# Scan step of a two-block layer: the state tile written in two quarters instead of whole through a mask

## Chip, cores and metric

The kernel runs on one core of a Trainium2 chip. The metric is the device time of one execution in microseconds; the kernel before has a median of 3163.56 us over three runs (3161.9 to 3165.33). One further execution was profiled; every row below is from it. Engine names are those of the profile: PE multiplies matrices (PEld is its weight load), DVE, ACT and POOL work elementwise, SP issues transfers.

## The reference, cut to what matters

The whole computation is two blocks of a network (feed-forward layers, convolutions, gating, retention). The change lies in one layer of the second block, the RWKV scan of 12 heads of width 64 over 768 tokens, in two directions:

```
def rwkv7_scan(r, w, k, v, kk, bb, s0, reverse):
    def step(s, inp):
        r_t, w_t, k_t, v_t, kk_t, b_t = inp
        sa = jnp.einsum('bhij,bhj->bhi', s, kk_t)
        s = s * w_t[:, :, None, :] - sa[..., None] * b_t[:, :, None, :] + v_t[..., None] * k_t[:, :, None, :]
        return s, jnp.einsum('bhij,bhj->bhi', s, r_t)
    ...
    s, ys = lax.scan(step, s0, xs, reverse=reverse)
```

Each head carries a 64 x 64 state `s` from token to token.

## The kernel before

`even_scan_phase` does the scan by chunks of 128 tokens (`CH`). Two heads share the 128 partitions: one head on partitions 0 to 63, the other on 64 to 127 (`SIDES`). There are six such pairs (`b` = 0 to 5, `RB` = 6), each with six chunks (`k` = 0 to 5, `NCH` = 6) and two directions (`d` = 0 and 1), so 36 steps of `step(b, k, between)` with both directions in each. The order of work is written out by hand: every engine has its own `step`, with the parts of direction 0 and 1 one after the other, and between them slots (`between(0)` to `between(5)`) into which the preparation of later pairs is put.

The state of a pair and direction is `V.sc` ("gathered" in the trace, 128 x 64: both heads stacked) and, for the products, `V.s` (a "state" tile in SBUF, 128 x 128): the two 64 x 64 blocks stand on its diagonal and the two other quarters are zero. On PE, `right` (L2900) and `read` (L2927) of the next step multiply with `V.s`. In the trace "state" is also the name of the PSUM tile `V.low`.

On DVE a step ends in this order: `join` for both directions (L3315, writes `V.x`), slot 3, `add` of direction 0 (L3325 on), `turn` of direction 0 and of direction 1 (L3321, a copy from PSUM to the half `early` of `V.t`: partitions 0 to 63 in direction 0, 64 to 127 in direction 1), `add` of direction 1, slots 4 and 5. `add` has three operations: the new `V.sc` (L3332, or a copy in L3334 at `k` = 0), the sum of the outputs (L3337), and after a wait for both the spread into `V.s` (L3339). PE's `close` (L2886) needs both `turn` copies of DVE and ACT's copy `y` (L3108); ACT's `close` (L3114) follows it, and PE's `take` of the next step (L2829) waits for that. PE's `tokens`, three copies on ACT (L3097 to L3100), and then `take` on DVE (L3296, "br") come next.

POOL works beside this for the next pairs: `prepare` with products of 128 x 768 (L2721), and `invert`, a chain of small products on 96 partitions (L2709, L2712), each waiting for the one before. It works for pairs 1 to 5, so it is nearly idle in the last pair.

Of the kernel before, what the change touches and what calls it, by code (L numbers as in the profile page):

```python
# [9 lines left out]
ALU = mybir.AluOpType  # L10
# [54 lines left out]
def at(i, n):  # L65

    return bass.ds(i, n)
# [2376 lines left out]
def even_scan_phase(K):  # L2444
# [7 lines left out]
    SIDES = (slice(0, 64), slice(64, 128))  # L2452
# [9 lines left out]
    with phase(K, "tables", "cleared", "late_ready", "late_out", *(f"gate_in{i}" for i in range(4)), "gate_hi", "gate_lo", "gate_lo_dve", "gate_done", "pp", "pa", "pd", "pq", "omk", "lw", "low_ps", "low_copied", "low_out0",  # L2462
# [23 lines left out]
        U = []  # L2486
# [23 lines left out]
        def heads(ap):  # L2510
            return ap.rearrange("p (a c) -> p a c", a=1).broadcast_to([P, 2, ap.shape[1]])

        def cols(d, k):
            return slice(ORDER[d][k] * CH, (ORDER[d][k] + 1) * CH)

        def total(b, k, signals, extra=0):

            return b * (NCH * signals) + (k * signals + extra)
# [53 lines left out]
        with nc.Block() as block:  # L2572
# [648 lines left out]
            def _(dve):  # L3221
# [103 lines left out]
                def add(b, k, d):  # L3325
                    O, V, way = B[b % 3], U[d], cols(d, k)
                    ch = ORDER[d][k]
                    dve.wait_ge(V.ps, total(b, k, PS, 4))
                    fresh = V.low[:, 3 * P:3 * P + 64]
                    if k:  # L3330
                        was = ORDER[d][k - 1]
                        new = dve.scalar_tensor_tensor(V.sc[:], V.sc[:], O.wlast[:, d, was:was + 1], fresh, ALU.mult, ALU.add)  # L3332
                    else:
                        new = dve.tensor_copy(V.sc[:], fresh)  # L3334
                    new.then_inc(V.ds, 1)
                    oc = u[:, at(b, 1), way].rearrange("p a t -> p (a t)")
                    dve.tensor_tensor(oc, oc, V.low[:, 2 * P:3 * P], ALU.add).then_inc(V.ds, 1)  # L3337
                    dve.wait_ge(V.ds, total(b, k, DS, 2))
                    dve.scalar_tensor_tensor(V.s.rearrange("p (h c) -> p h c", h=2), heads(V.sc), O.wlast[:, d, ch:ch + 1],  # L3339
                                             K.bd64.rearrange("p (h c) -> p h c", h=2), ALU.mult,  # L3340
                                             ALU.mult).then_inc(V.ds, 1)

                def begin():
                    dve.wait_ge(S.gate_done, GATES_DONE)
# [7 lines left out]
                def step(b, k, between):  # L3352
                    nxt = following(b, k)
                    take, keys, cross, join, turn = chunk_parts(nxt) if nxt else (lambda d: None,) * 5
                    if k == 0:
                        if b:
                            for d in range(2):
                                dve.wait_ge(U[d].ds, total(b, 0, DS))
                        dve.wait_ge(S.pd, prep("dve", b, "bonus"))
                    take(0)  # L3360
                    take(1)
                    between(0)
                    keys(0)
                    keys(1)
                    between(1)
                    cross(0)
                    cross(1)
                    between(2)
                    join(0)
                    join(1)  # L3370
                    between(3)
                    add(b, k, 0)
                    turn(0)
                    turn(1)
                    add(b, k, 1)
                    between(4)
                    between(5)
# [1341 lines left out]
```

## Time and profile before

| | |
|---|---|
| median of the runs | 3163.56 us |
| the profiled execution | 3161.93 us, of it span 3160.1 us |
| PE busy | 2982.9 us (94%), 22801 instructions |
| DVE busy | 2205.5 us (70%), 3864 instructions |
| ACT, POOL busy | 1387.2 us (44%), 1590.3 us (50%) |
| scan steps | 433 us, from 2241 to 2674 us of the span |
| L3339, the operation replaced | 72 times, 35.0 us |

The busy share of PE is high over the whole span, but many of its instructions in the scan are small products whose modelled lengths overlap. Which engine sets the pace of the scan is read from the waits and the order of time, not from the shares.

### The profile page before, as it was taken

The page shows a single profiled execution, that of the slowest core. Times are in us where ns is not written, and L with a number is a line of the kernel's source. Part 1 is how long each engine was busy: PE and PEld are TensorE (multiplying, and loading weights), DVE is VectorE, ACT ScalarE, POOL GpSimd, SP SyncE. Part 2 cuts the span into 40 slices and gives each one's busy share as a digit, 9 for nine tenths or more (in the row PEclk, how much of TensorE's full clock was granted, in tenths as well). Part 3 has the DMA queues.
Part 4 walks back from the last instruction along what each step waited for, and adds up shares of the span by engine and source line. Part 5 has one row for each costly group of instructions (what it writes and reads, how often), then busy time and mean ns, then how long its engine had stood idle before and what let it go on. Part 6 is the DMA issues. An engine that isn't in the chain of part 4 may idle for free. (4 is left out here: it accounts for less than half of the span.)

```text
span 3160.1 us, 57423 instructions
## 1 busy us (share of the span) xinstructions
PE 2982.9 (94%) x22801; PEld 2548.7 (81%) x22801; DVE 2205.5 (70%) x3864; ACT 1387.2 (44%) x2651; POOL 1590.3 (50%) x1197
## 2 busy tenths in 40 slices
PE   5999999899999999999999999999888899989998
PEld 4999876689987999877799888887666676778887
DVE  6998488799956999642799866447677764774443
ACT  4555235455524545234454524236444433444333
POOL 3776442367644775343477533224776660243333
PEclk8999999999999999999999999999899999999999
DMA  6565532246553564432345444214222243222222
GB/s 206 174 211 165 158 85 66 60 142 213 179 159 109 178 204 141 151 86 66 92 134 154 137 144 141 60 57 115 60 57 53 55 117 98 66 75 71 80 67 60
DMA packets 641459, 367.05 MB, mean 116 GB/s; under 512 B 107903, under 2 KB 634133, under 8 KB 640689
## 3 DMA queue, kind: packets, MB, share of 16 engines
q1 hardware_dynamic: 633216, 351.57, 38.0%
q10 hardware_dynamic: 6640, 10.49, 1.1%
q8 instruction: 176, 2.88, 0.4%
q0 software_dynamic: 1344, 1.44, 0.2%
q14 instruction: 83, 0.67, 0.1%
HBM read 334.27 MB, written 24.97 MB: 114 GB/s over the span
## 5 line engine op out<-in xcount | busy, mean ns | idle before, releaser
L270 POOL TENSOR_TENSOR w_lo<-w_raw,w_hi 128x1024 fp32r<-128x1024 f32 (+1 forms) x181 | 433.6, 2397 | 822.8 <-ACT w_hi L262 758.3
L262 ACT ACTIVATE w_hi<-w_raw 128x1024 fp32r<-128x1024 f32 (+1 forms) x172 | 175.1, 1018 | 364.1 <-PE acc L335 263.7
L1288 PE MATMUL scaled<-h_terms,h 128*128 128x256 f32 x1856 | 260.5, 283 | 0.0
L1288 PEld LDWEIGHTS scaled<-h_terms,h 128*128 128x128 f32 x1856 | 239.4, 192 | 0.0
L335 PE MATMUL acc<-h_terms,w_hi 128*128 128x512 f32 x584 | 220.0, 395 | 4.7 <-POOL w_lo L270 3.9
L978 DVE SCALAR_TENSOR_TENSOR ada_part<-ada_raw,c_act,ada_part 128x256 f32<-128x256 f32 x432 | 210.7, 488 | 16.1
L335 PE MATMUL acc<-hid,w_hi 128*128 128x512 f32 x528 | 206.1, 390 | 0.0
L335 PE MATMUL lat<-h,w_slots 128*128 128x512 f32 x672 | 199.5, 396 | 4.6 <-ACT plain L3967 4.0
L335 PE MATMUL acc<-h_terms,w_lo 128*128 128x512 f32 x520 | 203.3, 391 | 0.0
L668 DVE TENSOR_TENSOR scaled<-z,x 128x512 f32<-128x512 f32 x36 | 41.9, 1165 | 184.9 <-ACT z L609 184.9
L1135 POOL TENSOR_TENSOR h<-z,h 128x512 fp32r<-128x512 f32 x80 | 108.3, 1354 | 105.0 <-ACT h L1167 105.0
L335 PEld LDWEIGHTS lat<-h,w_slots 128*128 128x128 f32 x672 | 125.1, 188 | 33.1 <-ACT plain L3967 5.8
L1290 PE MATMUL scaled<-h_terms,h 128*128 128x256 f32 x928 | 149.2, 283 | 0.0
L270 POOL TENSOR_TENSOR w_slots<-w_raw,w_slots 128x1024 fp32r<-128x1024 f32 x28 | 68.9, 2459 | 159.5 <-ACT w_slots L262 153.1
L1135 POOL TENSOR_TENSOR w_lo<-w_sums,w_hi 128x512 fp32r<-128x512 f32 x72 | 93.7, 1301 | 103.4 <-ACT w_hi L1167 103.4
L1167 ACT ACTIVATE h<-w_raw 128x512 fp32r<-128x512 f32 x156 | 96.9, 624 | 103.5 <-PE scaled L1290 93.5
L335 PE MATMUL acc<-h,w_hi 128*128 128x512 f32 x408 | 134.9, 398 | 0.0
L335 PEld LDWEIGHTS acc<-h_terms,w_hi 128*128 128x128 f32 x584 | 110.1, 189 | 28.7 <-POOL w_lo L270 4.2
L1290 PEld LDWEIGHTS scaled<-h_terms,h 128*128 128x128 f32 x928 | 128.1, 192 | 0.0
L335 PEld LDWEIGHTS acc<-hid,w_hi 128*128 128x128 f32 x528 | 99.6, 189 | 19.4
L335 PEld LDWEIGHTS acc<-h_terms,w_lo 128*128 128x128 f32 x520 | 97.9, 188 | 20.9
L744 DVE SCALAR_TENSOR_TENSOR ada_part<-ada_raw,c_act,ada_part 128x256 f32<-128x256 f32 x240 | 109.8, 488 | 5.7
(789 smaller groups left out, 8826.4 us busy)
## 6 DMA issues: line engine op xcount, KB each, us to landing
w_raw<-in_ffn_w SPq DMA_DIRECT2D x240, 512.0 KB, 4.5
ada_raw<-in_ada_w SPq DMA_DIRECT2D x88, 1024.0 KB, 5.6
w_raw<-in_od_w_in SPq DMA_DIRECT2D x32, 512.0 KB, 4.1
w_raw<-in_ffn_w SPq DMA_DIRECT2D x32, 384.0 KB, 3.5
w_raw<-in_ev_w_in SPq DMA_DIRECT2D x22, 512.0 KB, 3.9
image<-inverse_wait SPq DMA_DIRECT2D x144, 64.0 KB, 2.1
first_ada<-in_ada_w SPq DMA_DIRECT2D x8, 1024.0 KB, 12.5
w_raw<-in_ab_w_in SPq DMA_DIRECT2D x16, 512.0 KB, 4.0
```

The source lines that it names most:

```text
L262: act.activation(K.w_hi[:, first % SPLIT, 0:tiles, :], K.raw[:, first % RAW, 0:tiles, :], ACT.Copy).then_inc(K.hi_ready, 1)
L270: pool.tensor_tensor(K.w_lo[:, first % SPLIT, 0:tiles, :], K.raw[:, first % RAW, 0:tiles, :], K.w_hi[:, first % SPLIT, 0:tiles, :].bitcast ...
L335: mm = pe.matmul(out, w[:, slot, k, :], moving(ap, k, tokens), start=first and k == 0 and p == 0, stop=last and k == tiles - 1 and p == le ...
L668: dve.tensor_tensor(S.tp[b % 2][:], K.z[:, b, :], K.x[:, b, :], ALU.mult).then_inc(S.crossed, 1)
L744: ins = dve.scalar_tensor_tensor(out, raw[:, k, :], col, part[:, v, :], ALU.mult, ALU.add)
L978: ins = dve.scalar_tensor_tensor(out, K.ada_raw[:, q % ADA, k, :], col, S.ada_part[:, v, :], ALU.mult, ALU.add)
L1135: pool.tensor_tensor(lo_of(t, p), full_of(t, p), hi_of(t, p).bitcast(F32), ALU.subtract).then_inc(S.lo, 1)
L1167: act.activation(hi_of(t, p), full_of(t, p), ACT.Copy).then_inc(S.hi, 1)
L1288: pe.matmul(out_of[p], hi_of(t, p)[:, k, :], moving[p][:, part, k, :], start=k == 0 and part == HI, stop=False)
L1290: mm = pe.matmul(out_of[p], lo_of(t, p)[:, k, :], moving[p][:, HI, k, :], start=False, stop=k == KH - 1)
```

## The change

The one masked operation L3339 on 128 x 128 elements (gathered state, taken twice, times decay, times the mask of ones and zeros `K.bd64`) becomes two operations on 64 x 64 elements, one for each head, each with its own decay and without a mask. In the first step of the scan each direction's `V.s` is set to zero once, and the first spread waits for that.

```diff
                     new.then_inc(V.ds, 1)
+                    if not b and not k:
+                        dve.memset(V.s[:], 0.0).then_inc(S.cleared, 1)
                     oc = u[:, at(b, 1), way].rearrange("p a t -> p (a t)")
                     dve.tensor_tensor(oc, oc, V.low[:, 2 * P:3 * P], ALU.add).then_inc(V.ds, 1)
                     dve.wait_ge(V.ds, total(b, k, DS, 2))
-                    dve.scalar_tensor_tensor(V.s.rearrange("p (h c) -> p h c", h=2), heads(V.sc), O.wlast[:, d, ch:ch + 1],
-                                             K.bd64.rearrange("p (h c) -> p h c", h=2), ALU.mult,
-                                             ALU.mult).then_inc(V.ds, 1)
+                    if not b and not k:
+                        dve.wait_ge(S.cleared, len(U) + d + 1)
+                    for a in SIDES:
+                        spread = dve.tensor_scalar(V.s[a, a], V.sc[a, :], O.wlast[a, d, ch:ch + 1], None, ALU.mult)
+                    spread.then_inc(V.ds, 1)
```

DVE around an `add` of both directions, before (pair 0, `k` = 4; `local40` and `local41` are `V.ds` of the two directions, `local30` and `local31` are `V.pa`, on which PE signals):

```order
L3337 TENSOR_TENSOR u<-u,state_561 128x128
L3339 SCALAR_TENSOR_TENSOR state<-gathered,w_last,const 128x128 [waits local40]
L3321 COPY t<-chunk_560 64x2x64 [waits local30]
L3321 COPY t<-chunk_571 64x2x64 [waits local31]
L3332 SCALAR_TENSOR_TENSOR gathered<-gathered,w_last,state_572 128x64 [waits local37]
L3337 TENSOR_TENSOR u<-u,state_572 128x128
L3339 SCALAR_TENSOR_TENSOR state<-gathered,w_last,const 128x128 [waits local41]
L3280 SCALAR_TENSOR_TENSOR x_context<-x_context,params,u 128x768 [waits local15]
L3296 TENSOR_TENSOR br<-chunk_560,masks 128x256 [waits local32]
```

The same place now:

```order
L3339 TENSOR_TENSOR u<-u,state_561 128x128
L3344 TENSOR_SCALAR state<-gathered,w_last 64x64 [waits local40]
L3344 TENSOR_SCALAR state<-gathered,w_last 64x64
L3321 COPY t<-chunk_560 64x2x64 [waits local30]
L3321 COPY t<-chunk_571 64x2x64 [waits local31]
L3332 SCALAR_TENSOR_TENSOR gathered<-gathered,w_last,state_572 128x64 [waits local37]
L3339 TENSOR_TENSOR u<-u,state_572 128x128
L3344 TENSOR_SCALAR state<-gathered,w_last 64x64 [waits local41]
L3344 TENSOR_SCALAR state<-gathered,w_last 64x64
L3280 SCALAR_TENSOR_TENSOR x_context<-x_context,params,u 128x768 [waits local15]
L3296 TENSOR_TENSOR br<-chunk_560,masks 128x256 [waits local32]
```

Nothing has moved; one operation has become two in each direction, and the second of them waits for nothing. Two `turn` copies stand behind the first pair of operations, and L3280 and `br` behind the second. Elsewhere the order is the same on every engine, but for the two clearing operations in the first step.

## Rows read from the trace of the kernel before

**Rows 1.** Busy time of each engine in the stretch of the scan steps

```profile
core 0: us, PE busy (x) PEld busy (x) DVE busy (x) ACT busy (x) POOL busy (x), PEclk, DMA share, GB/s
...
2241.00:2674.00 433.00, 378.61 (x6507) 284.87 (x6501) 288.42 (x682) 199.44 (x656) 257.65 (x353) 0.97 0.28 65
```

**Rows 2.** Waits in 2241 to 2673: waiter, releaser, total us, times, longest us

```profile
DVE br L3296 <- ACT tok L3100: 57.5, 54, 2.9
...
PE chunk L2886 <- DVE t L3321: 18.0, 31, 1.5
...
PEld state L2900 <- issue: 5.4, 29, 0.3
```

**Rows 3.** L3339 over the run: ns min/median/max; then busy us, mean ns

```profile
L3339 DVE SCALAR_TENSOR_TENSOR state<-gathered,w_last,const x72: 351/353/1678, 2241.5 to 2673.4; 128x128 f32<-128x128 f32 x72
...
L3339 DVE SCALAR_TENSOR_TENSOR state<-gathered,w_last,const 128x128 f32<-128x128 f32 x72 | 35.0, 486 | 2.6
```

**Rows 4.** Timeline (start us, us) of a step without POOL: DVE, then PE

```profile
2617.81 0.35 DVE L3339 SCALAR_TENSOR_TENSOR state<-gathered,w_last,const 128x128 f32<-128x128 f32 x1
2618.08 0.60 DVE L3321 COPY t<-chunk 64x128 f32<-64x128 f32 x2
...
2618.50 0.74 PE L2886 MATMUL chunk<-t,y 64*64 64x64 f32 x8 [0.21 <-DVE t L3321]
```

**Rows 5.** Pairs of DVE operations, timeline; and their mean ns by shape

```profile
2331.13 0.52 DVE L3315 TENSOR_TENSOR x<-image,chunk 128x128 f32<-128x128 f32 x2 [1.55 <-PE chunk L2864]
...
L3321 DVE COPY t<-chunk 64x128 f32<-64x128 f32 x72 | 20.5, 285 | 1.6 <-PE chunk L2877 0.4
...
L3315 DVE TENSOR_TENSOR x<-image,chunk 128x128 f32<-128x128 f32 x72 | 18.7, 287 | 35.7 <-PE chunk L2864 35.4
```

**Rows 6.** Single-input multiplications by a column elsewhere: busy us, mean ns

```profile
L3742 DVE TENSOR_SCALAR own_weights<-select,fac 128x32 f32<-128x32 f32 x2 | 0.4, 238 | 0.0
...
L3758 DVE TENSOR_SCALAR dft_lat<-sq,fac 128x256 f32<-128x256 f32 x1 | 0.3, 348 | 0.0
```

**Rows 7.** Timeline, a step with POOL's small products: DVE, POOL, PE

```profile
2254.10 0.61 DVE L3339 SCALAR_TENSOR_TENSOR state<-gathered,w_last,const 128x128 f32<-128x128 f32 x1
2254.63 0.60 DVE L3321 COPY t<-chunk 64x128 f32<-64x128 f32 x2
...
2253.96 0.60 POOL L2712 TENSOR_TENSOR w_raw<-w_raw,x 96x210 f32<-96x210 f32 x1
2254.64 0.59 POOL L2709 TENSOR_TENSOR x<-w_raw 96x220 f32<-96x220 f32 x1
...
2255.05 0.74 PE L2886 MATMUL chunk<-t,y 64*64 64x64 f32 x8 [0.97 <-DVE t L3321]
```

**Rows 8.** Timeline, a step with POOL's large products: DVE, then POOL

```profile
2292.35 1.56 DVE L3339 SCALAR_TENSOR_TENSOR state<-gathered,w_last,const 128x128 f32<-128x128 f32 x1
...
2295.64 2.57 DVE L3280 SCALAR_TENSOR_TENSOR x_context<-x_context,params,u 128x768 f32<-128x768 f32 x1
2298.13 0.74 DVE L3296 TENSOR_TENSOR br<-chunk,masks 128x256 f32<-128x256 f32 x2
...
2291.94 1.82 POOL L2721 TENSOR_TENSOR q_r_rate<-q_r_rate,x 128x768 f32<-128x768 f32 x1
2293.72 3.68 POOL L2721 TENSOR_TENSOR q_r_rate<-q_r_rate,u 128x768 f32<-128x768 f32 x2
```

**Rows 9.** Timeline of small operations outside the scan: DVE, then POOL

```profile
303.47 1.78 DVE L648 TENSOR_SCALAR fac<-mods 128x8 f32<-128x8 f32 x1
305.36 2.24 DVE L651 TENSOR_TENSOR fac<-fac,params 128x8 f32<-128x8 f32 x1
...
299.21 6.02 POOL L270 TENSOR_TENSOR w_lo<-w_raw,w_hi 128x768 fp32r<-128x768 f32 x1 [7.64 <-ACT w_hi L262]
...
305.19 2.38 POOL L270 TENSOR_TENSOR w_lo<-w_raw,w_hi 128x1024 fp32r<-128x1024 f32 x1
```

**Rows 10.** DVE's timeline behind the second direction's L3339 at k = 1

```profile
2335.32 1.76 DVE L3261 RECIPROCAL x_context<-x_context 128x128 f32<-128x128 f32 x2
2336.99 1.43 DVE L3243 TENSOR_TENSOR_SCAN q_r_rate<-dft_feat,q_r_rate 128x256 f32<-128x256 f32 x2
2338.34 0.90 DVE L3296 TENSOR_TENSOR br<-chunk,masks 128x256 f32<-128x256 f32 x2
```

## The prediction, made before the changed kernel was timed

> **What bounds the kernel now.** I read the busy time by stage first. The change touches only the scan steps: 433 us, in which DVE is busy 288 us [rows 1]. It is neither full nor idle, so the waits decide. In them PE's closing product L2886 waits in 31 of 35 steps for DVE's `turn` copy L3321, 18.0 us in all, while PE's first product with the spread state (L2900) never waits for DVE, only for 0.3 us at most of its own issue [rows 2]. So the spread state is always ready in time; what its making costs is that it stands in DVE's queue ahead of the `turn` copies. In a step without POOL the operation L3339 takes 0.35 us, the copies start 0.27 us after it began, and L2886 starts 0.42 us after them [rows 4]. With POOL at work L3339 takes 0.61 us, the copies start at 0.53 and L2886 at 0.95, again 0.42 after the copies [rows 7]. PE, then ACT, then PE's `take` and ACT's copies follow, and DVE itself waits 54 times for those copies before `br` [rows 2]. Time that direction 0's `add` gains or loses on DVE therefore goes into the step nearly whole. Direction 1's comes behind the copies and counts only where DVE has no rest before `br`.
>
> **What one operation costs now.** Alone 0.351 us; over 72 of them 35.0 us, so 35.0 - 72 x 0.351 = 9.7 us are waiting inside the operation [rows 3]. Of this 6.9 us fall to direction 0 (18 operations above 0.4 us, six of these above 0.7) and 2.75 us to direction 1. The cause is seen in the timelines: POOL's product ends at 2254.56, L3339 at 2254.71 [rows 7]; POOL's ends at 2293.76, L3339 at 2293.91 [rows 8]. Each time DVE's operation ends 0.15 us after POOL's: it has to wait until POOL is done, then streams its 128 columns. POOL starts its next product 0.08 us after the end of a small one [rows 7], and 0.04 us before the end of a large one [rows 8].
>
> **What two operations cost, alone.** The nearest rows for a single-input multiplication by a column are 0.238 us for 32 columns and 0.348 us for 256 [rows 6], half a ns a column; for 64 columns that is 0.25 us. (Bounds: 0.238 and 0.285, the latter a copy out of PSUM [rows 5].) Can the second start before the first has ended? Two `join` products of 0.287 us, both on all partitions, take 0.52 us together, so the second starts 0.05 us before the first ends; two `turn` copies of 0.285 us, the first written to the upper, the second to the lower 64 partitions, take 0.60 us, so there it starts 0.03 us after [rows 5 and 4]. The new pair changes halves as the `turn` copies do, and the first `turn` copy behind it changes back. I take the second case for both borders: 0.25 + 0.03 + 0.25 + 0.03 = 0.56 us from the start of the pair to the next operation, against 0.27 now: **+0.29 us** each time. By the first case it would be about 0.40, so +0.13.
>
> The Trainium skill, "VectorE: DVE Perf Modes", section "Two Vector instructions with no wait between them", states this as a rule: an instruction whose start quadrant (group of 32 partitions) differs from that of the last input or output in the same memory starts only when every earlier one has finished. The two pairs of rows agree, and by it both borders are held, as taken above; without it the sum below would be some 6 us less.
>
> **What two operations cost beside POOL.** The new ones read one tensor, L3339 read two. Do they still wait for POOL? Outside the scan a single-input multiplication of only 8 columns, L648, started at 303.47 and took 1.78 us; POOL's product ended at 305.23, L648 at 305.25. Behind it, after a wait for it, stands L651, again 8 columns: POOL had started its next product at 305.19, and L651 took 2.24 us, until 307.60, POOL's ending at 307.57 [rows 9]. So a small single-input operation is held up as well, and of two in a row **each is held up by a product of its own**: POOL takes its turn in between. In the new pair this does the following. The first ends 0.05 us after POOL's product (32 half-rate columns in place of 0.15 us); the second starts 0.03 later, when POOL has started its next one, and waits for its end, P later. Beside small products the next operation starts at end + 0.08 + P + 0.05 + 0.03, against end + 0.07 now: +0.09 + P. I put the pair in the place of each of the 72 operations in the timeline, with POOL's products as they lie there:
> - direction 0, 18 steps with POOL quiet or its product just over: 18 x 0.29 = 5.2 us;
> - direction 0, 14 steps with small products behind, P from 0.28 to 0.65 us (0.59 in [rows 7]), mean 0.53: 14 x 0.62 = 8.7 us;
> - direction 0, 4 steps with 1.82 us products behind [rows 8]: 4 x 1.81 = 7.3 us;
> - direction 1, only in the steps of pairs 0 to 3 where DVE has no rest before the next thing that is waited for: at `k` = 1, where reciprocals, scans and `br` follow without a gap [rows 10], 4 x 0.61 = 2.4; at `k` = 4, where `br` follows L3280 without one [rows 8], 4 x 1.91 = 7.7; at `k` = 5 4 x 0.29 = 1.2. Together 11.3 us. In the other 24 steps DVE waits for ACT before `br`, and that wait hides it; were the cover gone, at 0.29 each it would be 7 us more.
> - clearing: two writes of 128 columns, each under the 0.35 us of an operation that reads as many [rows 3], once: 0.3 us. The extra wait is on DVE's own clearing, with an operation in between.
>
> Sum: 5.2 + 8.7 + 7.3 + 11.3 + 0.3 = 32.8 us. Not all of it reaches the end: in some steps ACT is late by itself, and POOL's preparation does not move along, so a later step finds fewer products in its way. No row has this share; I take eight tenths, 26 us, with six tenths and the full sum (20 and 33) as ends. Against the profiled execution that is 3161.93 + 26 = 3188; that execution lies 1.6 us under the median of the runs, so I forecast **3190 us**.
>
> **The rivals.**
> *Held up once.* DVE's second operation might take its turn before POOL's next product: POOL's start and the second operation's fall together, at end + 0.08. Then every pair costs 0.29: 48 x 0.29 = 13.9, by the same share some 11 us: 3175. Against it stands L651 [rows 9], though POOL had there a start of 0.17 us.
> *Not held up at all.* The two lose the second tensor, and if that is what POOL collides with, the waiting of 9.7 us goes. Direction 0: 36 x 0.29 - 6.9 = 3.5; direction 1 in the 12 steps: 3.5 - 2.65 = 0.9; clearing 0.3: +4.7 us, 3168, not to be told from no change. L648 speaks against it [rows 9].
> The Trainium skill, "SBUF — State Buffer", section "Who interferes with whom", says that a DVE instruction with at most one SBUF input does not contend with GpSimd outside the two-port modes, and that single-input multiplications can enter such a mode and then take the shared pair for the whole instruction. The 0.5 ns a column of rows 6 (two elements in a cycle of the page's 0.96 GHz) speaks for that mode here.
> *Faster.* Not held up and not held at the change of halves either: about 0.20 us a pair decides it, since 48 pairs then give back 9.6 us in all. At two starts 0.17 us apart (0.34 in all, +0.07): 48 x 0.07 - 6.9 - 2.65 = -6 us, 3157. Both the copies of rows 5 and L648 would have to mislead.
>
> **How the numbers follow.** A measurement of this kernel tells about 0.2%, 6.3 us, from no change. Held up twice 0.66 (3180 to 3203), held up once 0.13 (3172 to 3180), not held up 0.13 (3164 to 3172), faster 0.05, and more than the full sum 0.03. The third case is within 0.2% but for 0.01 below it. Slower 0.82, same 0.12, faster 0.06. The range from 3167 to 3203 leaves out the faster case, the lower end of the case not held up and the tail above.
>
> **What would show it.** In the profile after, L3344 has 144 operations; alone 0.25 us; beside POOL some of up to 1.9 us, and their sum well over 35 us (near 36 + 30). In a quiet step `turn` starts 0.56 us after the pair. L2886 waits for L3321 for some 35 us in place of 18.0. The scan's stretch grows from 433 to about 459 us, and nothing outside it changes. Wrong it would be if no operation of L3344 is over 0.3 us (not held up), if only every first is (held up once), or if the longer pair stands while the stretch does not grow: then the wait for L3321 was not the one that counts.

## The result and the profile after

The changed kernel takes 3183.96 us (median of four runs, 3183.31 to 3186.17) against 3164.18 us before (four runs, 3161.9 to 3165.33): ratio 1.0066, 95% interval 1.0054 to 1.0079, so 19.8 us slower. The profiled execution took 3183.31 us, span 3181.5 us.

The replaced operation in the profile after, first by its summary over the run (ns min/median/max), then by busy us and mean ns, answering [rows 3]:

```profile
L3344 DVE TENSOR_SCALAR state<-gathered,w_last x144: 246/254/1764, 2244.8 to 2696.6; 64x64 f32<-64x64 f32 x144
```
```profile
L3344 DVE TENSOR_SCALAR state<-gathered,w_last 64x64 f32<-64x64 f32 x144 | 62.5, 434 | 3.6
```

Alone an operation takes 0.25 us, as forecast from [rows 6]. All 144 take 62.5 us in place of 35.0; 62.5 - 144 x 0.25 = 26.5 us of it are waiting, against 9.7 before.

A quiet step after, DVE and then PE (start us, us), answering [rows 4]:

```profile
2638.70 0.52 DVE L3344 TENSOR_SCALAR state<-gathered,w_last 64x64 f32<-64x64 f32 x2
2639.25 0.61 DVE L3321 COPY t<-chunk 64x128 f32<-64x128 f32 x2
```
```profile
2639.68 0.74 PE L2886 MATMUL chunk<-t,y 64*64 64x64 f32 x8 [0.49 <-DVE t L3321]
```

The copies start 0.55 us after the pair (0.27 before), PE's closing product 0.43 us after them, having waited 0.49 (0.21 before).

A step with POOL's large products after: DVE's two operations one by one, then POOL, answering [rows 8]:

```profile
2299.06 1.64 DVE L3344 TENSOR_SCALAR state<-gathered,w_last 64x64 f32<-64x64 f32 x1
```
```profile
2300.72 1.75 DVE L3344 TENSOR_SCALAR state<-gathered,w_last 64x64 f32<-64x64 f32 x1
```
```profile
2298.86 1.80 POOL L2721 TENSOR_TENSOR q_r_rate<-q_r_rate,x 128x768 f32<-128x768 f32 x1
2300.62 3.56 POOL L2721 TENSOR_TENSOR q_r_rate<-q_r_rate,u 128x768 f32<-128x768 f32 x2
```

POOL's product ends at 2300.66, the first operation at 2300.70. The second starts at 2300.72, when POOL has begun its next at 2300.62. The last row is two POOL products; by half of its 3.56 us the first of them ends at some 2302.4, and the second operation ends at 2302.47. So each operation was held up by a product of its own.

Waits in 2241 to 2700 after (total us, times, longest), answering [rows 2]:

```profile
PE chunk L2886 <- DVE t L3321: 36.4, 31, 3.4
...
POOL x L2721 <- DVE x_context L3261: 16.5, 4, 10.0
...
PEld state L2900 <- issue: 6.4, 29, 0.3
```

PE's closing product waits 36.4 us for the copies in place of 18.0; the product with the state tile still waits for nothing but its own issue. POOL now waits 16.5 us for DVE's reciprocals; before it was 1.9.

Where the 21.4 us between the spans lie: from the first to the last `add` of direction 0 the scan takes 450.5 us in place of 431.1, +19.4. It starts 3.2 us later (2244.27, before 2241.05), ahead of any changed operation, and what follows is 1.2 us shorter. In the twelve kernels below the same place lies between 2240.97 and 2249.46, so that start is not an effect of the change. Outside the scan the executions of these kernels take from 2729.0 us (before: span 3160.1 less the 431.1 in the table) to 2735.6 (psum) and 2739.8 (the pair in the other order), so a few us between two totals can lie there; the table shows the scan alone. The table sums the steps of pairs 0 to 3 by `k`, then pairs 4 and 5, each from one `add` of direction 0 to the next in the profiled executions (us); the kernels of the last five columns are described below.

| steps | before | changed | pair_d0 | pair_d1 | psum | late_after | on_act |
|---|---|---|---|---|---|---|---|
| k = 0 | 50.1 | 51.7 | 51.9 | 50.6 | 51.4 | 50.0 | 50.3 |
| k = 1 | 54.9 | 62.3 | 63.7 | 58.8 | 57.3 | 65.0 | 53.8 |
| k = 2 | 53.2 | 54.2 | 54.5 | 52.6 | 52.5 | 52.7 | 60.3 |
| k = 3 | 46.7 | 43.1 | 43.6 | 42.5 | 46.7 | 39.5 | 42.4 |
| k = 4 | 57.7 | 67.1 | 66.4 | 66.2 | 49.9 | 76.1 | 47.8 |
| k = 5 | 59.4 | 61.0 | 57.6 | 56.2 | 59.0 | 59.2 | 52.2 |
| pair 4 | 63.9 | 64.3 | 65.7 | 63.6 | 63.6 | 61.5 | 63.3 |
| pair 5 | 45.3 | 46.8 | 46.8 | 45.4 | 47.2 | 44.9 | 48.2 |
| sum | 431.1 | 450.5 | 450.1 | 435.7 | 427.6 | 448.9 | 418.2 |

### The profile page after: what moved, and what is told of

Read it like the earlier page. It is cut to its first block and busy times, and to the rows that moved or that the text cites. A ratio compares the mean times of both kernels' runs of the same rounds, so it can differ in the third digit from the quotient of the medians.

```text
span 3181.5 us, 57499 instructions
## 1 busy us (share of the span) xinstructions
PE 2992.3 (94%) x22801; PEld 2556.1 (80%) x22801; DVE 2235.8 (70%) x3938; ACT 1388.4 (44%) x2651; POOL 1587.4 (50%) x1197
## 3 DMA queue, kind: packets, MB, share of 16 engines
q0 software_dynamic: 1344, 1.44, 0.2%
## 5 line engine op out<-in xcount | busy, mean ns | idle before, releaser
L335 PEld LDWEIGHTS acc<-hid,w_hi 128*128 128x128 f32 x528 | 99.7, 189 | 19.4
```

The costliest lines, as they stand in the source:

```text
L335: mm = pe.matmul(out, w[:, slot, k, :], moving(ap, k, tokens), start=first and k == 0 and p == 0, stop=last and k == tiles - 1 and p == le ...
```

## The experiments

My theory: each of the two operations is held up by a product of POOL, and these hold-ups and 0.28 us of issue lengthen the step through the copies behind them. The rivals: that two operations cost by their issue alone; that the place in the queue is what counts; that TensorE's clock is part of it. Ratios are to the kernel before, run beside each.

**Away from POOL: the operand from PSUM.**

```diff
-                        spread = dve.tensor_scalar(V.s[a, a], V.sc[a, :], O.wlast[a, d, ch:ch + 1], None, ALU.mult)
+                        spread = dve.tensor_scalar(V.s[a, a], fresh[a, :], O.wlast[a, d, ch:ch + 1], None, ALU.mult)
```

> Both operations of the pair kept, but they read the chunk's new part from PSUM in place of the gathered state in SBUF (the state carried over from earlier chunks is left out of the spread tile). Theory that the pair is held up because it reads SBUF through what it shares with POOL: no operation is over 0.33 us, pair to copy 0.62 us everywhere, against 0.55 quiet and up to 3.4 beside POOL in the changed kernel. Sum against the kernel before: 36 x 0.35 - 6.9 + 12 x 0.35 - 2.65 = +7 us, 3171 (3166 to 3175). Rival, that two operations one behind the other are what costs by their issue and the waits behind: 3184 as the changed kernel, or above.

3164.77 us, ratio 1.0008 (0.9999 to 1.0017). The 144 operations over the run:

```profile
L3344 DVE TENSOR_SCALAR state<-state,w_last x144: 275/284/293, 2246.6 to 2675.6; 64x64 f32<-64x64 f32 x144
```

Each takes 0.03 us more than in the changed kernel and none is over 0.293 us, beside the same POOL work. Two operations, one behind the other, and almost nothing is lost: without hold-ups by POOL the loss is gone. What two cost alone is still there (pair 5, with POOL quiet, takes 47.2 us in place of 45.3), and it is given back at k = 4, where the four steps shrink to 49.9 us, below the 57.7 before. The hold-ups of the old masked operation are gone there too; by my sum that would be some 2.4 us, and L3280 takes 1.75 to 1.94 us there in place of 2.57. The time lies 6 us under what I expected, most of it at k = 4; why L3280 comes out shorter I did not test. The Trainium skill, "VectorE: DVE Perf Modes", section "Why PSUM operands drop a tier", says that the mode that reads through both SBUF ports is impossible with a PSUM operand; the trace agrees with that, with 293 ns at most against 1764, but does not show the mode itself.

**One operation in place of two.**

```diff
-                    for a in SIDES:
-                        spread = dve.tensor_scalar(V.s[a, a], V.sc[a, :], O.wlast[a, d, ch:ch + 1], None, ALU.mult)
+                    spread = dve.tensor_scalar(V.s[:, 0:64], V.sc[:], O.wlast[:, d, ch:ch + 1], None, ALU.mult)
```

> One single-input multiplication of all 128 partitions by 64 columns in the place of the pair; it writes only the left half of the state tile, so the right head's block is left out of the computation. Held-up-once-for-each-operation theory: it takes 0.25 us alone and can be held up by one product of POOL only; it ends 0.1 us earlier than the masked operation both alone and beside POOL, and the copies behind it start 0.17 us after it when POOL is quiet. Time 3160 (3157 to 3164). Rival, that the single-input mode beside POOL is what costs, however many operations there are: some operations over 1 us remain in the steps with small products, time 3172 or more.

3160.43 us, ratio 0.9994 (0.9985 to 1.0003).

```profile
L3343 DVE TENSOR_SCALAR state<-gathered,w_last 128x64 f32<-128x64 f32 x72 | 28.7, 399 | 2.6
```

Waiting: 28.7 - 72 x 0.25 = 10.7 us, as the masked operation's 9.7 and far from 26.5. One operation is held up as one was before; a quiet step takes 9.86 us in place of 9.96. The number of operations makes the loss, not their kind.

**A third operation.**

```diff
-                    for a in SIDES:
-                        spread = dve.tensor_scalar(V.s[a, a], V.sc[a, :], O.wlast[a, d, ch:ch + 1], None, ALU.mult)
+                    for a, c in zip((*SIDES, SIDES[0]), (*SIDES, SIDES[1])):
+                        spread = dve.tensor_scalar(V.s[a, c], V.sc[a, :], O.wlast[a, d, ch:ch + 1], None, ALU.mult)
```

> A third operation of the same kind behind each pair; it writes a quarter of the state tile that has to stay zero, so the result of the scan is another. Theory that each operation of its own is held up by one product of POOL: a quiet pair grows from 0.52 to 0.79 us, beside POOL the third ends one product later (1.1 to 1.7 us, 3.4 to 5.2), the operation's waiting over all is 1.5 to 1.7 times that of the changed kernel (26.5 us), and the time grows by about as much again as the second did: 3200 (3195 to 3208). Rival, that POOL is held up no more than twice since it has then caught up: only 72 x 0.27 us of issue, by the share of 0.6: 3192 or less.

3202.51 us, ratio 1.0123 (1.0108 to 1.0138): 39.6 us over the kernel before, twice the 19.8 of the pair.

```profile
L3344 DVE TENSOR_SCALAR state<-gathered,w_last 64x64 f32<-64x64 f32 x216 | 97.1, 449 | 4.7
```
```profile
2298.66 3.78 DVE L3344 TENSOR_SCALAR state<-gathered,w_last 64x64 f32<-64x64 f32 x3
```

Waiting: 97.1 - 216 x 0.25 = 43.1 us, 1.6 times that of the pair. At k = 4 direction 0's three take 5.3 to 5.4 us in pairs 1 to 3, one product more than two. In pair 0 (the row of 3.78 us) the first was held up by none (0.26 us) and the other two by one product each (1.75 and 1.74); in direction 1 of pairs 0 to 3 one of the three went free each time. In a quiet step the three take 0.78 us. So "one product each" is what most of these rows show, with exceptions.

**One direction at a time.** The pair in direction 0 or 1, the masked operation in the other:

```diff
+                    if d == 0:
                         for a in SIDES:
                             spread = dve.tensor_scalar(V.s[a, a], V.sc[a, :], O.wlast[a, d, ch:ch + 1], None, ALU.mult)
+                    else:
+                        spread = dve.scalar_tensor_tensor(...)
```

> The pair of operations in direction 0 alone, the masked operation kept in direction 1. The prediction's sum gives direction 0 21.3 of 32.8 us; the changed kernel's +19.8 us is 0.6 of the sum, so by the same share 13 us here: 3176. Rival, that direction 1 costs nothing because DVE waits before br anyway: the whole +20, 3183.

> The pair in direction 1 alone. By the sum 11.3 of 32.8 us, with the same share +7 us: 3170. Rival, direction 1 hidden: 3163. What is left over or missing when both halves are added is what the two directions hide or cause in one another.

Direction 0 alone: 3184.55 us, ratio 1.0068 (1.0053 to 1.0082), +21.7 us, all of the loss. Direction 1 alone: 3168.59 us, ratio 1.0018 (1.0009 to 1.0027), +5.7 us. Both rivals have half the truth: direction 1's pair is not hidden by itself, yet it adds nothing to direction 0's. At k = 4 either one lengthens the four steps from 57.7 to some 66 us, and both together to 67.1. The traces show why. With direction 1's pair alone, in 2241 to 2700:

```profile
PE prep L2772 <- DVE x_context L3280: 6.5, 4, 1.9
```

L2772 is PE's product for the next pair. At k = 4 it stands in PE's queue ahead of the `take` (L2829) that goes on with the scan, and it needs what L3280 writes. That `take` follows it without a gap in all four steps of the kernel before, the changed one and these two, and `br` had ended at least 0.9 us earlier: `br` is not what the step waits for there. Direction 1's pair makes L3280 late; direction 0's makes PE itself late, since the closing product waits for the copies. L2772 starts when the later of the two is done. With direction 0's pair alone it never waits for L3280 at k = 4, with both it waits 2.2 us in three steps. So the two delays cover each other.

**The pair in other orders.** First the lower half before the upper one (`for a in SIDES[::-1]`), then both on the upper half:

```diff
                     for a in SIDES:
-                        spread = dve.tensor_scalar(V.s[a, a], V.sc[a, :], O.wlast[a, d, ch:ch + 1], None, ALU.mult)
+                        spread = dve.tensor_scalar(V.s[SIDES[0], a], V.sc[SIDES[0], :], O.wlast[SIDES[0], d, ch:ch + 1], None, ALU.mult)
```

> The pair in the other order: the lower 64 partitions first, the upper ones last, so that direction 0's turn copy, which writes the upper ones, changes no half. Theory that an operation on another half starts only after the one before has ended: the copy starts 0.08 us earlier than in the changed kernel (0.47 in place of 0.55 us after the pair's start in quiet steps), 36 x 0.08 = 2.9 us and as much again in the steps where DVE has no rest: 3180 (3178 to 3183). Rival, no such rule: 3184, copy at 0.55.

> Both operations of the pair on the upper 64 partitions (the right head's blocks are left out of the state tile, the left head's is written twice, into two quarters). Theory that the change of half makes the second operation wait for the end of the first: here it starts 0.08 us before that end, the pair takes 0.42 to 0.45 us in place of 0.52, the copy starts 0.34 to 0.38 us after the pair's start in place of 0.55, a quiet step is 10.05 us (before 9.96, changed kernel 10.24). Beside small products of POOL the second operation asks before POOL's next and is held up less often; beside large ones as before. Time 3168 to 3174. Rival, no such rule: pair 0.52, time 3184.

Quiet steps of the two, DVE:

```profile
2672.34 0.52 DVE L3344 TENSOR_SCALAR state<-gathered,w_last 64x64 f32<-64x64 f32 x2
2672.78 0.60 DVE L3321 COPY t<-chunk 64x128 f32<-64x128 f32 x2
```
```profile
2676.04 0.41 DVE L3344 TENSOR_SCALAR state<-gathered,w_last 64x64 f32<-64x64 f32 x2
2676.37 0.60 DVE L3321 COPY t<-chunk 64x128 f32<-64x128 f32 x2
```

From the pair's start to the copies 0.55 us in the changed kernel, 0.44 with one border fewer, 0.33 with none: each change of half costs 0.11 us, in place of the 0.08 I took. The quiet steps follow, 10.24, 10.13 and 10.02 us. The times follow only in part. Reversed took 3175.69 us (3166.22 to 3179.96, a wide spread), ratio 1.0035 (1.0022 to 1.0049). That is under my range of 3178 to 3183 and 8 us under the changed kernel, where 36 x 0.11 explains 4; the rest stays open. Both on one half took 3179.0 us, ratio 1.005 (1.0035 to 1.0065), 5 us over the top of what I expected: k = 1 and k = 4 are short (53.0 and 54.2 us), but k = 3 and k = 5 take 60.5 and 67.4. At k = 5 the second operation of direction 0 is now held up, and takes 1.83 us in pairs 1 to 3. At k = 3 the pair is not what costs (0.48 us at most for one operation) but a wait of ACT, first in the kernel before, then here:

```profile
ACT w_raw L3087 <- POOLq L2714: 5.5, 3, 2.9
```
```profile
ACT w_raw L3087 <- POOLq L2714: 15.1, 4, 5.5
```

L3087 is ACT's copy of what POOL's chain `invert` has made. At k = 3 it stands in ACT's queue ahead of the copies L3097 to L3100 that the scan needs, and all these waits lie at k = 3. In the changed kernel it is one wait of 0.3 us.

**The place in the queue.** The spread of direction 0 behind the two copies, in the kernel before and in the changed one (`spread` is what stood at the end of `add`, made a function; its definition is left out here):

```diff
                     add(b, k, 0)
                     turn(0)
                     turn(1)
+                    spread(b, k, 0)
                     add(b, k, 1)
+                    spread(b, k, 1)
```

> The kernel before with its masked operation, only that direction 0's is moved behind the two turn copies. Theory that its place ahead of the copies is what counts: the copies start 0.27 us earlier in quiet steps and up to 1.5 us beside POOL, but PE's closing product gains no more than it waited for them (0.21 in quiet steps), and where DVE has no rest nothing is gained. 24 steps with 0.2 to 0.5 us: -8 us, 3156 (3150 to 3160). Rival, that DVE's work as a whole counts and not its place: 3164, no change.

> The changed kernel with direction 0's pair moved behind the two turn copies, direction 1's where it was. Theory that the place ahead of the copies makes the cost: quiet steps 9.78 us as in the kernel before with its masked operation moved (changed kernel 10.24), PE's closing product waits under 10 us for DVE (36.4); what is left is the steps where DVE has no rest: 4 x 2 to 3 us at k = 4 and 4 x 1 at k = 1 against the kernel before. Time 3171 (3166 to 3177). Rival, that the hold-ups cost the same wherever the pair stands: 3184.

With the masked operation 3161.83 us, ratio 0.9996 (0.9987 to 1.0005), no difference that can be told; with the pair 3182.85 us, ratio 1.0062 (1.0046 to 1.0077), the same as where it stood. The quiet steps do what the theory says: both take 9.78 us (before 9.96, changed 10.24), and the closing product waits 3.3 us in all for L3321. It is given back at k = 4. Direction 1's pair there, with direction 0's moved, and PE's first product with that state tile (L3348 is what L3344 is in the changed kernel):

```profile
2300.84 2.98 DVE L3348 TENSOR_SCALAR state<-gathered,w_last 64x64 f32<-64x64 f32 x2
```
```profile
2303.87 0.70 PE L2900 MATMUL state<-state,q_r_rate 128*64 128x128 f32 x4 [2.85 <-DVE state L3348]
```

Direction 0's pair (2.77 us) and direction 1's (2.98) stand on DVE with only two short operations between them, and L3280 (2.50) follows. The copies are out early, so PE comes early, and then it waits for the state tile itself, 2.7 to 2.9 us in each of the four steps, and 1.5 us more in each for what L3280 writes; the four steps take 76.1 us. In the kernels before and changed no wait of PE for the state tile is over 0.1 us. So the wait for the copies is the way of the loss in quiet steps; at k = 4, beside POOL's large products, the loss finds another way when that one is taken from it: the state tile, and L3280 ahead of PE's L2772.

**TensorE's clock.** The granted clock in the scan (the third number from the end in a row of busy times) in the changed kernel; before it was 0.97 [rows 1]:

```profile
2241.00:2696.00 455.00, 391.55 (x6557) 295.20 (x6556) 319.72 (x757) 200.94 (x656) 255.32 (x353) 0.94 0.27 62
```

A mean of 0.94 between the levels of 2.4 and 1.2 GHz is 12% of the time at the lower one, 55 us; 0.97 of the 433 us before is 26 us. So the clock was at its lower level about twice as long. At k = 4 of pair 0 it fell after the closing product had waited 3.38 us: the 16 products of L2829 there, at 1.2 GHz, last 1.56 us, and 0.89 in the same place before, at 2.4. The prediction did not have this term. The test, ahead of PE's closing products:

```diff
+                    if b < 4 and k in (1, 4):
+                        pe.wait_ge(U[0].aa, total(*nxt, AA, 5))
+                        for n in range(12):
+                            pe.matmul(U[0].wide[:, 0, 0:64], K.ident, K.ident[:, 0:64], start=True, stop=True)
```

> The changed kernel with twelve products on PE, whose result nobody reads, ahead of its closing products in the eight steps k = 1 and k = 4 of pairs 0 to 3, where PE waits longest for DVE. Theory that part of the loss is TensorE's granted clock, which is at 1.2 GHz more often in the changed kernel's scan (mean 0.94 against 0.97): with PE busier in these waits the mean goes back to 0.96 or more, and the time falls by 3 to 7 us, to 3179. Rival, that the clock is not part of it: 3184 to 3188, the products costing what they last beyond the wait.

```profile
2241.00:2690.00 449.00, 397.86 (x6683) 302.83 (x6681) 319.63 (x752) 198.74 (x652) 255.08 (x353) 0.98 0.27 63
```

The clock is back, at 0.98, and the time is 3181.5 us (3180.78 to 3185.06), ratio 1.0061 (1.0048 to 1.0075), against 1.0066 (1.0054 to 1.0079). In the profiled executions the scan takes 447.9 us in place of 450.5. A difference of 0.0005 is not to be told from nothing, and each interval is some 4 us wide on either side. The added products also cost something at k = 4 (68.2 us in place of 67.1), so a share of the clock of a few us is neither shown nor excluded; the bulk of the loss stays with the clock back, so it is not the main cause.

**The spread on ACT.** DVE loses the operation; ACT writes the blocks behind its `close`, and DVE's next `add` waits for that:

```diff
+                    def spread(d):
+                        O, V, ch = B[b % 3], U[d], ORDER[d][k]
+                        act.wait_ge(V.ds, total(b, k, DS, 2))
...
+                        for a in SIDES:
+                            ins = act.activation(V.s[a, a], V.sc[a, :], ACT.Copy, scale=O.wlast[a, d, ch:ch + 1])
+                        ins.then_inc(V.ds, 1)
...
                     close(0)
                     close(1)
+                    spread(0)
+                    spread(1)
```

> Both blocks are written by two copies with a scale on ACT for each direction, behind ACT's close; DVE has no spread at all. Theory: the copies on DVE come 0.27 us and more earlier, DVE has 0.27 to 2 us less in the steps where it has no rest, ACT's four copies of some 0.2 us fit into its wait of 1.2 us before the next chunk's copies, and POOL holds up none of them. 3148 (3142 to 3155). Rival, that ACT is then late for the next chunk's copies: the wait of 1.2 us is gone and each step is 0.1 to 0.5 us longer, 3164 to 3180.

3152.36 us, ratio 0.997 (0.9961 to 0.9979): 10.8 us faster than the kernel before and some 30 faster than the changed one. ACT in a quiet step:

```profile
2633.80 1.44 ACT L3135 ACTIVATE state<-gathered,w_last 64x64 f32<-64x64 f32 x4
```

The four copies last 1.44 us (342 to 352 ns each over the run, POOL beside or not) where a quiet ACT had 1.2 us of waiting (I had taken some 0.2 us for each copy), and the step is 10.05 us in place of 9.96: the rival's effect, 0.1 us. At k = 4 the four steps take 47.8 us in place of 57.7. At k = 2 ACT's own work makes them longer, 60.3 in place of 53.2: the four copies stand there ahead of the copies that `br` waits for, in a queue without a rest. To halve ACT's load, direction 0 alone was given to it and direction 1 kept DVE's masked operation:

```diff
-                    spread(1)
+                    if d:
+                        dve.wait_ge(V.ds, total(b, k, DS, 2))
+                        dve.scalar_tensor_tensor(V.s.rearrange("p (h c) -> p h c", h=2), heads(V.sc), O.wlast[:, d, ch:ch + 1],
...
```

> Direction 0's two blocks are written on ACT behind its close, direction 1's tile by DVE's masked operation as in the kernel before. A quiet step: the copies on DVE come earlier as with the masked operation moved (9.78 us), and ACT has two copies of 0.35 us in a wait of 1.2 us, in place of the four that made the quiet step 10.06. In the steps where DVE has no rest it loses direction 0's operation alone. Time 3151 (3147 to 3156), against 3152 with both directions on ACT. Rival, that the masked operation of direction 1 beside POOL costs more than the four copies save: 3158.

3158.18 us, ratio 0.999 (0.9981 to 0.9999), the rival's number. Quiet steps are 9.78 us as expected, but the 36 operations left on DVE take 21.5 us, 0.598 each, against 35.0 for all 72 before; and ACT's L3087 waits 5.7 us for POOL's chain again, which it did not with both directions on ACT. That these two make the difference is argued, not shown. The profiled execution (3153.05 us) is the fastest of the eleven, 5 us under their median.

## Why the prediction was right, and where not

The direction and the range held: 3190 forecast, 3167 to 3203 the range, 3184 measured; +26 us forecast, +19.8 measured. So did the mechanism on DVE, two hold-ups in place of one. The way from there to the end of the step was right for direction 0 and wrong for direction 1 at k = 4, and the nearness of the sum is in part luck.

- *What two cost alone*: 0.25 us each and +0.29 us a pair; measured 0.246 to 0.254 and +0.28 in pair 5, where all five steps grow by 0.28 to 0.32 us. The step passes it on whole. The hold at the change of halves is there (0.11 us a border).
- *Held up twice*: seen in single rows, and by psum, one and triple. The rivals "held up once" and "not held up" are out.
- *The sum, step by step* (pairs 0 to 3; the forecast is my placing of the 36 steps at the full sum, of which the prediction gives only the totals): k = 1 5.1 forecast, 7.4 measured; k = 2 2.8 and 1.0; k = 3 1.7 and -3.6; k = 4 13.4 and 9.4; k = 5 3.9 and 1.6. In the sum itself 4 x 1.81 is 7.2, not 7.3, and 1.81 and 1.91 stand for POOL products of one kind without a reason; neither matters.
- *The mis-sized term is direction 1's*, 11.3 us. Alone it measured 5.7, on top of direction 0's nothing. Its largest part, 4 x 1.91 at k = 4, rested on `br` following L3280 without a rest. `br` does, but PE's `take` did not wait for it: the way runs from L3280 to PE's L2772, and there direction 0's delay covers most of it (2.2 us of waiting left in the changed kernel). In pair 0 L3280 was not held up either:

```profile
2306.03 1.02 DVE L3280 SCALAR_TENSOR_TENSOR x_context<-x_context,params,u 128x768 f32<-128x768 f32 x1
```

  It took 2.57 us before [rows 8] and came now just as POOL was between two products; the pair had taken that wait on itself. In pairs 1 to 3 it still took 2.50 us.
- *Direction 0's 21.2 us* (5.2 + 8.7 + 7.3) came out as 21.7 when it was alone, with no eight tenths. That agreement is luck: in the table its steps at k = 1 and k = 4 grow by 17.5 us where I had 8.4, and those at k = 3 and k = 5 shrink by 4.9 where I had 4.4 more. So the share of 0.60 of the full sum, the lower end I had given it, is not a share by which each step passes its loss on.
- *k = 3*: I had no gain there. In the kernel before, ACT's L3087 waits 5.5 us in three of these steps for the end of POOL's chain; in the changed kernel, which comes to them later, it waits 0.3 us. That is 5.2 us less waiting in steps that became 3.6 us shorter. With both operations on one half it waits 15.1 us, 9.6 more, and the steps are 13.8 us longer. POOL's preparation, which does not move along with the scan, gives back a part of what is lost elsewhere. The prediction said that POOL's preparation does not move along, but gave this no number.
- *What would show it*: L3344 "near 66 us" was 62.5, the wait for L3321 "some 35" was 36.4, the scan "459" was 452 (433 + 19.4).

## What to carry to other kernels

Splitting one DVE operation into two smaller ones beside a busy POOL is not priced by elements: count how many separate operations in a row POOL can hold up, each time by one of its products, and by how long those are. Look for an engine or an operand that POOL does not meet (here ACT, or PSUM as the source) before making the operation shorter. And add up such waits only up to the next operation that would have waited itself: find the instruction that the next engine really waits for (here PE's L2772 behind L3280, and ACT's L3087 behind POOL's chain, and not `br`), since two delays that meet there do not add.

## What the runs showed of the hardware that I had not expected

An operation of DVE (64x64, one tensor read) with its input in PSUM was not held up by POOL in any of 144 cases (293 ns at most), the same with its input in SBUF up to 1764 ns. A change between the two halves of the partitions costs DVE 0.11 us at each border. TensorE's granted clock was 0.94 in the mean over the changed kernel's scan, with waits of PE of up to 3.4 us for the copies, against 0.97 before, where the longest was 1.5; twelve products ahead of eight of the closing products brought it to 0.98, and no difference in time could be told (ratio 1.0061 and 1.0066).
